# Seven block products instead of eight for half of the values and two thirds of the keys' and values' projection

## The chip, the cores and the metric

The kernel runs on one core of a Trainium2 chip. The metric is the device time of one execution in microseconds; a profiled execution lists every instruction of each engine. TensorE (PE) multiplies, VectorE (DVE) and ScalarE (ACT) do elementwise work, SyncE (SP) issues most DMAs.

## The reference

One inference step of a two-layer decoder trunk in float32: 512 prompt tokens and 8 x 4 sample tokens, 544 in all, with a model width of 1024. Layer one is a gated MLP, layer two attends to keys and values projected once. Two products matter here:

```
uv = gelu(rmsnorm(x) @ w_in)            # w_in 1024 x 4096; the last 2048 columns are the values v
v  = layernorm(v, ln_g, ln_b)           # over the 2048 columns, so after all of them are there
y  = (u * spatial(v)) @ w_out           # the mixing
...
kv = rmsnorm(h, kv_norm) @ kv_w         # kv_w 1024 x 1536: three branches of keys and values
proj = rmsnorm(h) @ b_w_in              # the queries, next after the keys
```

## The kernel before

Every float32 operand is split into a high part (ScalarE writes it, type fp32r) and a low part (VectorE subtracts the high part), and a product is three matmuls: high x high, high x low, low x high. The weights are loaded in items into two slots (`raw`), and split into `wh` and `wl`. `w_hi` and `w_ready` count high parts and finished items; `w_ready` begins at 2, so item n is finished at n + 3.

The values (lines 962 to 964) and the keys (1141 to 1143) are made token-major. `pair_b` (line 779) takes 512 columns of the weights: two items of 4 k rows, four tiles of 128 tokens, for each tile 8 k x 3 matmuls of 128x512 (line 786) into one of six PSUM banks. The 32 sample tokens go another way: four partial products in one bank (line 796), split, and gathered by a selector into bank `WIDE_GATHER` (line 805). The first half of a pair is done for all four tiles, then the second, so each tile is complete some time before the next. ScalarE scales each tile into `vt` (with Gelu) or `kvtok` (line 1669), then the few tokens (1672), then makes the high part of the next item (1653). VectorE splits (2161, the values' statistics 2192). The values have four pairs, the keys three, and the queries follow as pairs 3 and 4 with the same counters.

After the values VectorE aggregates the statistics (2351), and the mixing starts: TensorE's `mix_in` items (line 754) and `mix_spatial` (1004), VectorE's scaling (2369), finishing of `vt` (2389, 2394) and gating (2378 and `store`), ScalarE's normalising (1767). TensorE's first mixing item has in its middle the transposes of the spatial weights `wsraw` (976).

The order on every engine is written out by hand. The counters that the change touches are `f_mm` (partial products done), `wide_mm` (tiles done), `wide_free` and `wide_few` (tiles and few tokens stored), `k_sq`, `k_sd` (used for the keys' head squares).

## Time and profile before

| | us |
|---|---|
| median of 3 runs | 1540.78 |
| lowest run | 1538.75 |
| the profiled execution | 1539.93 |
| its span, from the first to the last instruction | 1538.1 |
| TensorE busy in it | 1508.9 |
| VectorE busy | 1051.4 |
| ScalarE busy | 640.4 |

In the profile an instruction's duration runs to its completion, and one may start a little before the last has ended, so the time from start to start is what an engine's queue pays. Matmuls overlap in the same way: a 128x512 one is listed with 0.39 us and the next starts after 0.23.

### The profile page before, as it was taken

To read this page: it belongs to the slowest core of one execution; us is meant where nothing else is said; L and a number is where in the kernel's file an instruction comes from. 1 tells how busy PE (TensorE), PEld (TensorE's weight loads), DVE (VectorE), ACT (ScalarE), POOL (GpSimd) and SP (SyncE) were. 2 spreads that over 40 slices of the span, in tenths; PEclk is the share of its full clock that TensorE was granted. 3 is DMA by queue.
4 is the path that set the end of the run, shared out by engine and by line. 5 is a ranking of instruction groups with operands and counts; after the bars stand their busy time and mean duration, and the time that the engine had idled before them with its cause. 6 is when DMAs were issued, how large, how long until landed. Compare 5 with 4: busy or idle time off the path is not lost.

```text
span 1538.1 us, 28834 instructions
## 1 busy us (share of the span) xinstructions
PE 1508.9 (98%) x11746; PEld 1380.4 (90%) x11746; DVE 1051.4 (68%) x1567; ACT 640.4 (42%) x1067; POOL 94.5 (6%) x155
## 2 busy tenths in 40 slices
PE   9999999999999999999999999998999999999998
PEld 6779999999999999998777756776799999999998
DVE  5339753368877869756266777877668969778952
ACT  6335311233333324334344667776543334333422
POOL 0000000000000000000000125553000000000000
PEclk9999999999999999999999999999999999999999
DMA  5438222322231323232315613104542232323232
GB/s 171 159 105 300 63 83 83 100 82 83 69 121 58 124 91 95 76 110 82 110 61 159 175 57 110 56 1 140 153 121 83 69 96 83 110 69 124 81 101 69
DMA packets 127816, 157.09 MB, mean 102 GB/s; under 512 B 11930, under 2 KB 102386, under 8 KB 127282
## 3 DMA queue, kind: packets, MB, share of 16 engines
q1 hardware_dynamic: 127346, 155.29, 31.7%
q8 instruction: 83, 1.36, 0.4%
q14 instruction: 35, 0.29, 0.1%
q10 hardware_dynamic: 352, 0.15, 0.0%
HBM read 149.58 MB, written 14.16 MB: 106 GB/s over the span
## 4 chain that ended last, share of the span: by engine, by line
PE 91%; DVE 5%; ACT 2%; issue 1%; DMA 0%; POOL 0%; SPq 0%; DVEq 0%; ACTq 0%
PE PS L754 40%; PE PS L1067 21%; PE PS L786 13%; PE PS L1383 2%; PE PS L1398 2%; PE PS L1300 2%; PE PS L1355 1%; PE PS L796 1%; PE PS L1263 1%; PE PS L1004 1%; PE PS L1366 1%; DMA xtok<-in_x_prompt 0%; PE PS L1518 0%; PE PS L1495 0%; PE PS L1461 0%
## 5 line engine op out<-in xcount | busy, mean ns | idle before, releaser
L2161 DVE TENSOR_TENSOR wl<-raw,wh 128x2048 fp32r<-128x2048 f32 (+2 forms) x89 | 167.9, 1887 | 128.4 <-ACT wh L1653 85.1
L1633 ACT ACTIVATE wh<-raw 128x2048 fp32r<-128x2048 f32 (+2 forms) x73 | 110.4, 1513 | 227.7 <-PE PS L754 140.5
L2212 DVE TENSOR_TENSOR hT<-PS,hT 128x544 f32<-128x544 f32 (+1 forms) x104 | 75.1, 722 | 130.4 <-PE PS L754 130.0
L1067 PE MATMUL PS<-opL,whA 128*128 128x272 f32 x512 | 148.7, 290 | 0.0
L1067 PE MATMUL PS<-opH,whA 128*128 128x272 f32 x512 | 147.8, 289 | 0.4 <-DVE wlB L2477 0.4
L1067 PE MATMUL PS<-opH,wlA 128*128 128x272 f32 x512 | 147.8, 289 | 0.0
L754 PE MATMUL PS<-act0h,wh 128*128 128x272 f32 x640 | 133.5, 290 | 0.4 <-DVE sg L2369 0.4
L754 PE MATMUL PS<-act0l,wh 128*128 128x272 f32 x640 | 132.3, 288 | 0.0
L754 PE MATMUL PS<-act0h,wl 128*128 128x272 f32 x640 | 132.3, 288 | 0.0
L1067 PE MATMUL PS<-opL,whB 128*128 128x272 f32 x384 | 111.5, 290 | 0.0
L1067 PE MATMUL PS<-opH,wlB 128*128 128x272 f32 x384 | 110.8, 289 | 0.0
L1067 PE MATMUL PS<-opH,whB 128*128 128x272 f32 x384 | 110.7, 288 | 0.0
L754 PEld LDWEIGHTS PS<-act0h,wh 128*128 128x128 f32 x640 | 100.5, 188 | 0.8 <-issue 0.5
L754 PEld LDWEIGHTS PS<-act0h,wl 128*128 128x128 f32 x640 | 100.3, 188 | 0.0
L754 PEld LDWEIGHTS PS<-act0l,wh 128*128 128x128 f32 x640 | 100.3, 188 | 0.0
L1067 PEld LDWEIGHTS PS<-opH,whA 128*128 128x128 f32 x512 | 96.7, 189 | 0.8 <-DVE wlB L2477 0.8
L1067 PEld LDWEIGHTS PS<-opH,wlA 128*128 128x128 f32 x512 | 96.5, 189 | 0.0
L1067 PEld LDWEIGHTS PS<-opL,whA 128*128 128x128 f32 x512 | 96.2, 188 | 0.0
L754 PE MATMUL PS<-f1h,wh 128*128 128x272 f32 x448 | 92.8, 288 | 0.0
L754 PE MATMUL PS<-f1h,wl 128*128 128x272 f32 x448 | 92.8, 289 | 0.0
L754 PE MATMUL PS<-f1l,wh 128*128 128x272 f32 x448 | 92.4, 288 | 0.0
L786 PE MATMUL PS<-wh,act0h 128*128 128x512 f32 x224 | 89.4, 399 | 1.1 <-DVE act0l L2312 1.1
(416 smaller groups left out, 3688.6 us busy)
## 6 DMA issues: line engine op xcount, KB each, us to landing
raw<-in_ffn_w_gate SPq DMA_DIRECT2D x44, 512.0 KB
raw<-in_ffn_w_up SPq DMA_DIRECT2D x44, 512.0 KB
raw<-in_a_w_in SPq DMA_DIRECT2D x32, 512.0 KB, 4.7
raw<-in_ffn_w_down SPq DMA_DIRECT2D x64, 256.0 KB
raw<-in_a_w_out SPq DMA_DIRECT2D x16, 512.0 KB
crows<-in_cache_kv_cmp SPq DMA_DIRECT2D x32, 256.0 KB, 2.9
cache<-in_state_kv_win SPq DMA_DIRECT2D x8, 1024.0 KB, 7.5
out_kv_win_sample<-in_state_kv_win SPq DMA_DIRECT2D x8, 1016.0 KB
```

The lines of the kernel that those rows point to most:

```text
L754: mm = pe.matmul(PS[:, 4 * ps + 2 * mt + h, 0:HALF], W[:, rs, k, mt * P:mt * P + P], Xp[:, k * T + h * HALF:k * T + h * HALF + HALF], star ...
L786: return pe.matmul(PS[:, wide_bank(QT * w + t), :], Xp[:, a:a + P], wide(W, k // 4)[:, k % 4, :], start=(k == 0 and W is wh and Xp is xh), ...
L796: mm = pe.matmul(PS[32 * j:32 * j + 32, WIDE_FEW, :], few[:, 4 * half + j, :], wide(raw, half)[:, j, :], start=(half == 0), stop=(half == 1))
L1004: pe.matmul(PS[:, 4 + 2 * mt, ch * P:ch * P + P], vt[:, ch, f0:f0 + P], wsT[:, g, :], start=False, stop=(ch == QT - 1))
L1067: mm = pe.matmul(PS[:, bank, 0:HALF], w, X[:, x, k, :], start=(k == 0 and not last and X is opH), stop=(k == 3 and last))
L1263: tr = pe.transpose(PS[:, 2 * (m % 2) + p, pg * P:pg * P + P], rows, ident)
L1300: mm = pe.matmul(PS[:, 4 + y % 2, 0:n], W2[:, y % 2, l, :], x[:, :, l, :], start=(l == 0), stop=(l == 7))
L1383: tr = pe.transpose(PS[:, 5 + n % 3, c0 + kt * P:c0 + kt * P + P], probs_at(v, g2)[:, kt * P:kt * P + P], ident)
L1398: mm = pe.matmul(PS[64 * g2:64 * g2 + 64, 4, 0:P], kvtok[:, kt, c0:c0 + HD], turned_at(v, g2)[:, kt * P:kt * P + P], start=(br == 0 and kt ...
L1633: act.activation(wh[:, rs, 0:kn, :], raw[:, rs, 0:kn, :], ACT.Copy).then_inc(w_hi, 1)
L2161: dve.tensor_tensor(wl[:, rs, 0:kn, :], raw[:, rs, 0:kn, :], wh[:, rs, 0:kn, :].bitcast(F32), ALU.subtract).then_inc(w_ready, 1)
L2212: dve.tensor_tensor(h, psum_u(s, mt), h, ALU.add).then_inc(free[s], 1)
```

## The change

The last 1024 columns of the values (pairs 2 and 3) and of the keys' projection (pairs 1 and 2) become one `unit` each: a 512 x 1024 by 1024 x 1024 product, cut into 2 x 2 blocks (256 tokens by 512 k, 512 k by 512 columns), made with seven block products in Winograd's form instead of eight. `unit_b` does them on TensorE as items 0 to 7; the product with the fourth input sum is done as two half items, 4 and 5.

- Four sums of input blocks (`unit_sums_made`, VectorE; high parts `unit_sums_high`, ScalarE; low parts `unit_sum_low`, VectorE). The sums are made ahead: for the values after the first pair's splits, for the keys ahead of the first.
- Four sums or differences of weight blocks, called T1 to T4 after their counter values, made by VectorE in place in `raw` and in two more buffers (`r2`), then split as items.
- Seven joins on VectorE that add results in PSUM to what stands in `vt` or `kvtok`: U2, U4, C12, C22, U3, C11, C21. Product 0 is copied out by ScalarE. ScalarE then applies Gelu (or the scaling) in place to the joined blocks.
- The unit's weights: block 0 in four DMAs, a second block into `r2`, a third into slot 1, and the last one after product 3's operand is split. The load of `wsraw` is moved behind the first two mixing items.
- The few tokens keep partial products and gathers, with the same numbers; the first four are issued inside the pair ahead (`unit_first_few`), the next eight write the gather bank and so wait for `wide_few`.
- The counters of items, `k_sq` and `k_sd` are shifted for everything later.

```diff
-    at_v = plan.take(8, 0)
+    at_v = plan.take(12, 0)
...
+    unit_v = unit_of(at_v[0] + 4, 2 * QT, 4, 2, 4, 0, vt, 1024, 0, few_v, part_v, sel_v,
+                     (A_P1, A_P1 + 8192, A_P2 + 17408, A_P2 + 25600), r2_at(0, A_P1 + 16384, A_P1 + 20480), (2, 4, 0))
+    unit_k = unit_of(at_kv[0] + 2, V_TILES + QT, 10, 5, 10, 1, kvtok, 512, 32, few_k, part_b, sel_b,
+                     tuple(A_V + 8192 * j for j in range(4)), r2_at(1, A_P2 + 30720, A_SG), (4, 2, 0))
...
+        def unit_blocks(u, w, c):
+            sp.wait_ge(w_ready, u.item + 1)
+            sp.wait_ge(f_mm, u.few_mm - 1)
+            block([wide(raw, 0)[:, k:k + 1, :] for k in range(4)], w, 0, c, loaded[0], 64)
+            block([x[:, :, :] for x in u.r2], w, 0, c + 2 * CW, s_first, 32)
+            sp.wait_ge(w_ready, u.item + 2)
+            sp.wait_ge(f_mm, u.few_mm)
+            block([wide(raw, 1)[:, 2 * j:2 * j + 2, :] for j in range(2)], w, 4, c + 2 * CW, loaded[1], 32)
+        def unit_last_block(u, w, c):
+            sp.wait_ge(w_ready, u.item + 3 + 3)
+            sp.wait_ge(f_mm, u.few_mm + 3)
+            block([wide(raw, 1)[:, 2 * j:2 * j + 2, :] for j in range(2)], w, 4, c, loaded[1], 96)
...
+        def unit_first_few(u):
+            pe.wait_ge(w_ready, u.item + 3)
+            for j in range(4):
+                mm = pe.matmul(PS[32 * j:32 * j + 32, WIDE_FEW, :], u.few[:, j, :], wide(raw, 0)[:, j, :], start=True, stop=False)
+            mm.then_inc(f_mm, 1)
...
+            def product(item, X, bank, ks=range(4), slot=0, after=None):
+                pe.wait_ge(w_ready, u.item + item + 3)
+                s = item % 2
+                for t in range(2):
+                    for k in ks:
+                        for Xp, W in ((X[0], wh), (X[0], wl), (X[1], wh)):
+                            mm = pe.matmul(PS[:, bank + t, :], Xp(k, t), wide(W, s)[:, k - slot, :],
+                                           start=(k == 0 and W is wh and Xp is X[0]), stop=(k == 3 and Xp is X[1]))
+                    if t == 0 and after is not None:
+                        after()
+                mm.then_inc(wide_mm, 1)
...
+            pe.wait_ge(s_first, u.second + 64)
+            pe.wait_ge(wide_few, u.few_n)
+            partials(WIDE_GATHER, 0, lambda j: u.r2[j // 2][:, j % 2, :], True)
+            pe.wait_ge(loaded[1], 32 * u.item + 64)
+            partials(WIDE_GATHER, 1, lambda j: wide(raw, 1)[:, j, :], False)
+            pe.wait_ge(wide_free, u.stored - (u.item == unit_v.item) * QT)
+            product(0, block(0, 0), a)
+            pe.wait_ge(wide_free, u.stored)
+            product(1, made(0), b)
+            product(2, made(1), c)
+            pe.wait_ge(wide_free, u.stored + 1)
+            product(3, made(3), a, after=lambda: gather(0))
+            pe.wait_ge(k_sq, u.joins + U4)
+            product(4, made(2), b, ks=range(2))
+            product(5, made(2), b, ks=range(2, 4), slot=2)
+            pe.wait_ge(loaded[1], 32 * u.item + 256)
+            partials(WIDE_FEW, 1, lambda j: wide(raw, 1)[:, j, :], False)
+            product(6, block(1, 0), c)
+            pe.wait_ge(k_sq, u.joins + U3)
+            product(7, block(1, 1), b, after=lambda: gather(1))
...
-        for w in range(4):
-            pair_b(w, at_v, (act0, few_v, part_v, sel_v), 0, 0, 0,
-                   *((first_values, values_split, values_few) if w == 0 else ()))
+        pair_b(0, at_v, (act0, few_v, part_v, sel_v), 0, 0, 0, first_values, values_split, values_few)
+        pair_b(1, at_v, (act0, few_v, part_v, sel_v), 0, 0, 0, ahead=unit_v)
+        unit_b(unit_v)
...
+            pe.wait_ge(k_sq, unit_v.joins + C21)
             pe.wait_ge(wide_few, 4)
             spread_and_turn()
-        pe.wait_ge(wide_free, V_TILES - 2)
+        pe.wait_ge(k_sq, unit_v.joins + C11)
...
-        for w in range(3):
-            pair_b(w, at_kv, (act0, few_k, part_b, sel_b), 8, V_TILES, 4,
-                   *((first_keys, keys_split, keys_few) if w == 0 else ()))
+        pair_b(0, at_kv, (act0, few_k, part_b, sel_b), 8, V_TILES, 4, first_keys, keys_split, keys_few, ahead=unit_k)
+        unit_b(unit_k)
...
+        def unit_sums_high(u):
+            act.wait_ge(k_sq, u.joins + MADE)
+            for j in range(4):
+                ins = act.activation(u.S[j][0][:, :, :], u.x_sum[j], ACT.Copy)
+            ins.then_inc(k_sd, 1)
...
+            act.wait_ge(k_sq, u.joins + T1)
+            unit_split(u, 1, r0, 0)
+            few_high(WIDE_GATHER, u.few_mm + 3)
+            act.wait_ge(k_sq, u.joins + T2)
+            unit_split(u, 2, r0, 1)
+            act.wait_ge(f_lo, u.few_mm + 2)
+            act.activation(u.dst[:, 0:2, c1:c1 + 512], PS[:, a:a + 2, :], ACT.Copy).then_inc(wide_free, 1)
+            act.wait_ge(loaded[1], 32 * u.item + 64)
+            unit_split(u, 3, r1, 2)
+            act.wait_ge(k_sq, u.joins + T3)
+            act.wait_ge(wide_mm, u.tiles + 3)
+            act.activation(wide(wh, 0)[:, 0:2, :], u.r2[0][:, :, :], ACT.Copy).then_inc(w_hi, 1)
+            act.wait_ge(wide_mm, u.tiles + 4)
+            act.activation(wide(wh, 1)[:, 0:2, :], u.r2[1][:, :, :], ACT.Copy).then_inc(w_hi, 1)
+            act.wait_ge(loaded[1], 32 * u.item + 256)
+            unit_split(u, 6, r1, 5)
+            few_stored(0, c2)
+            stored(C12, 0, c2, 2)
+            few_high(WIDE_FEW, u.few_mm + 4)
+            act.wait_ge(k_sq, u.joins + T4)
+            act.wait_ge(wide_mm, u.tiles + 6)
+            for j in range(2):
+                ins = act.activation(wide(wh, 1)[:, 2 * j:2 * j + 2, :], u.r2[j][:, :, :], ACT.Copy)
+            ins.then_inc(w_hi, 1)
+            stored(C22, 1, c2, 2)
+            after(0)
+            stored(C11, 0, c1, 2)
+            few_stored(1, c1)
+            stored(C21, 1, c1, 1)
+            after(1)
...
+                if u is not None and p == pairs - 1:
+                    act.wait_ge(loaded[0], 32 * u.item + 256)
+                    act.wait_ge(wide_done, 2 * (p0 + p) + 1)
+                    act.activation(wide(wh, 0), wide(raw, 0), ACT.Copy).then_inc(w_hi, 1)
+                else:
+                    wide_split(0, at[0] + 2 * p + 2, wide_done, 2 * (p0 + p) + 1)
+                if u is not None and p == pairs - 1:
+                    unit_sums_high(u)
...
+            for k0 in range(0, 4, 2):
+                for k in range(k0, k0 + 2):
+                    for n, (i, j) in enumerate(((1, 1), (0, 0))):
+                        link.put(dve.tensor_scalar(u.x_part[:, 2 * (k - k0) + n, :], x(i, j, k), g(j, k), None, ALU.mult))
+                link.settle()
+                for k in range(k0, k0 + 2):
+                    fused(s1, 1, 0, k, u.x_part[:, 2 * (k - k0), :], ALU.add)
+                    fused(s3, 1, 0, k, u.x_part[:, 2 * (k - k0) + 1, :], ALU.subtract)
+                link.settle()
+                for k in range(k0, k0 + 2):
+                    fused(s2, 0, 0, k, s1[:, k, :], ALU.subtract)
+                link.settle()
+                for k in range(k0, k0 + 2):
+                    fused(s4, 0, 1, k, s2[:, k, :], ALU.add)
+                link.settle()
+            dve.memset(small[:, 1, 3:4], 0.0).then_inc(k_sq, 1)
...
+            unit_sum_low(u, 0)
+            dve.wait_ge(f_mm, u.few_mm + 1)
+            dve.wait_ge(s_first, u.second + 64)
+            dve.wait_ge(w_ready, u.item + 3)
+            for j in range(2):
+                half = dve.tensor_tensor(r0[:, 2 * j:2 * j + 2, :], u.r2[j][:, :, :], r0[:, 2 * j:2 * j + 2, :], ALU.subtract)
+            half.then_inc(k_sq, 1)
+            low(1, r0)
+            dve.wait_ge(w_ready, u.item + 4)
+            dve.wait_ge(loaded[1], 32 * u.item + 64)
+            joined(r0, r0, r1, ALU.subtract, T2)
+            unit_sum_low(u, 1)
+            few_low(WIDE_GATHER, u.few_mm + 2)
+            low(2, r0)
+            for j in range(2):
+                half = dve.tensor_tensor(u.r2[j][:, :, :], u.r2[j][:, :, :], r1[:, 2 * j:2 * j + 2, :], ALU.subtract)
+            half.then_inc(k_sq, 1)
+            unit_sum_low(u, 3)
+            low(3, r1)
+            unit_sum_low(u, 2)
+            dve.wait_ge(wide_mm, u.tiles + 3)
+            dve.wait_ge(wide_free, u.stored + 1)
+            joined(m2, c, m1, ALU.add, U2)
+            joined(u4, b, m2, ALU.add, U4)
+            low(4, u.r2[0][:, :, :], 2)
+            dve.wait_ge(w_ready, u.item + 4 + 3)
+            dve.wait_ge(loaded[1], 32 * u.item + 256)
+            dve.tensor_tensor(u.r2[0][:, :, :], r0[:, 0:2, :], r1[:, 0:2, :], ALU.add)
+            dve.wait_ge(wide_mm, u.tiles + 4)
+            joined(m3, a, u4, ALU.add, C12)
+            low(5, u.r2[1][:, :, :], 2)
+            dve.wait_ge(w_ready, u.item + 5 + 3)
+            joined(u.r2[1][:, :, :], r0[:, 2:4, :], r1[:, 2:4, :], ALU.add, T4)
+            low(6, r1)
+            dve.wait_ge(wide_mm, u.tiles + 6)
+            joined(u4, b, u4, ALU.add, C22)
+            joined(m2, b, m2, ALU.add, U3)
+            few_low(WIDE_FEW, u.few_mm + 4)
+            dve.wait_ge(w_hi, u.item + 7 + 1)
+            for j in range(2):
+                ins = dve.tensor_tensor(wide(wl, 1)[:, 2 * j:2 * j + 2, :], u.r2[j][:, :, :],
+                                        wide(wh, 1)[:, 2 * j:2 * j + 2, :].bitcast(F32), ALU.subtract)
+            ins.then_inc(w_ready, 1)
+            stat(1, (2,), (0, 1), 1)
+            dve.wait_ge(wide_mm, u.tiles + 7)
+            joined(m1, c, m1, ALU.add, C11)
+            split(0, u.item + 8)
+            stat(1, (2,), (2, 3), 3)
+            stat(0, (), (0, 1), 5)
+            dve.wait_ge(wide_mm, u.tiles + 8)
+            joined(m2, b, m2, ALU.add, C21)
+            stat(0, (1,), (2, 3), 7)
+            split(1, u.item + 9)
```

## Rows read from the trace of the kernel before

**Rows 1.** The page: busy time and share, then the chain by engine.

```profile
PE 1508.9 (98%) x11746; PEld 1380.4 (90%) x11746; DVE 1051.4 (68%) x1567; ACT 640.4 (42%) x1067; POOL 94.5 (6%) x155
...
PE 91%; DVE 5%; ACT 2%; issue 1%; DMA 0%; POOL 0%; SPq 0%; DVEq 0%; ACTq 0%
```

**Rows 2.** The chain of waits in the values: start us, us, engine and line.

```profile
64.42 19.65 PE PS L786 x84
...
84.53 2.80 PE PS L786 x12
...
112.11 6.04 PE PS L754 x48
```

**Rows 3.** The chain of waits, the keys and the queries.

```profile
732.52 1.85 PE PS L796 x16
...
782.07 1.85 PE PS L796 x16
...
818.28 0.49 PE PS L1162 x5
```

**Rows 4.** Busy time by stretch: length, PE, PEld, DVE, ACT, POOL, PEclk, DMA share, GB/s.

```profile
62.57:112.11 49.54, 49.54 (x230) 37.46 (x231) 17.51 (x26) 15.06 (x16) 0.00 (x0) 1.00 0.48 162
...
732.52:782.07 49.55, 49.55 (x232) 37.20 (x236) 10.37 (x6) 14.64 (x16) 0.00 (x0) 1.00 0.25 85
...
132.83:159.88 27.05, 26.64 (x216) 26.32 (x215) 26.57 (x42) 6.76 (x9) 0.00 (x0) 1.00 0.71 233
...
900.00:1000.00 100.00, 94.66 (x845) 65.11 (x843) 79.53 (x158) 66.85 (x190) 48.56 (x65) 1.00 0.25 85
```

**Rows 5.** The timeline of VectorE after the values: start us, us, instruction.

```profile
115.25 2.29 DVE L2161 TENSOR_TENSOR wl<-raw,wh 128x2048 fp32r<-128x2048 f32 x1 [0.97 <-ACT wh L1653]
...
117.46 1.99 DVE L2351 BATCH_NORM_AGGREGATE stats<-bstat 128x2 f32<-128x48 f32 x5
...
126.08 0.72 DVE L2369 TENSOR_TENSOR sg<-PS,rsb 128x544 f32<-128x544 f32 x1 [0.16 <-PE PS L754]
...
132.83 0.72 DVE L2369 TENSOR_TENSOR sg<-PS,rsb 128x544 f32<-128x544 f32 x1 [1.26 <-PE PS L754]
```

**Rows 6.** Groups of instructions, shapes kept apart: busy us, mean ns, idle before.

```profile
L2161 DVE TENSOR_TENSOR wl<-raw,wh 128x2048 fp32r<-128x2048 f32 x53 | 121.7, 2297 | 117.1 <-ACT wh L1653 85.1 <-ACT wh L1633 32.0
...
L2161 DVE TENSOR_TENSOR wl<-raw,wh 128x1024 fp32r<-128x1024 f32 x32 | 39.2, 1224 | 7.5 <-ACT wh L1633 7.5
...
L1633 ACT ACTIVATE wh<-raw 128x1024 fp32r<-128x1024 f32 x32 | 34.0, 1061 | 147.1 <-PE PS L1067 86.1 <-PE PS L754 61.0
...
L2312 DVE SCALAR_TENSOR_TENSOR act0l<-hT,gains,act0h 128x256 fp32r<-128x256 f32 x4 | 1.9, 480 | 0.0
```

**Rows 7.** The timelines of VectorE and ScalarE around the values' second pair.

```profile
53.06 2.29 DVE L2161 TENSOR_TENSOR wl<-raw,wh 128x2048 fp32r<-128x2048 f32 x1 [8.92 <-ACT wh L1653]
...
63.33 1.41 DVE L2192 BATCH_NORM_STATS2 bstat<-vt 128x6 f32<-128x256 f32 x4 [2.48 <-ACT vt L1669]
...
62.61 0.69 ACT L1669 ACTIVATE vt<-PS,stats 128x512 f32<-128x512 f32 x1 [2.54 <-PE PS L786]
...
63.19 0.68 ACT L1672 ACTIVATE vt<-PS,stats 128x512 f32<-128x512 f32 x1
```

**Rows 8.** The timelines of VectorE and ScalarE in the keys.

```profile
719.27 0.19 DVE L2285 RECIPROCAL stats<-stats 128x5 f32<-128x5 f32 x1 [0.28 <-ACT stats L1704]
...
729.54 2.29 DVE L2161 TENSOR_TENSOR wl<-raw,wh 128x2048 fp32r<-128x2048 f32 x1 [4.46 <-ACT wh L1653]
...
785.21 2.29 DVE L2161 TENSOR_TENSOR wl<-raw,wh 128x2048 fp32r<-128x2048 f32 x1 [10.38 <-ACT wh L1653]
...
727.59 1.92 ACT L1653 ACTIVATE wh<-raw 128x2048 fp32r<-128x2048 f32 x1 [3.33 <-DMA raw<-in_kv_w]
```

**Rows 9.** DMA issues of the first 140 us: KB each, median us to landing.

```profile
raw<-in_a_w_in SPq DMA_DIRECT2D x26, 512.0 KB, 4.7
...
wsraw<-in_a_w_spatial SPq DMA_DIRECT2D x1, 512.0 KB, 9.8
```

More of the change, by code:

```diff
@@ L812, in tile_free @@
                     pe.wait_ge(wide_free, i0 + i - 5)
+                if behind is not None and t % 2 == 0:
+                    pe.wait_ge(k_sq, behind.joins + (C11, C21)[t // 2])
             if first is None:
@@ new lines, in unit_wide, with few_high, few_stored, stored @@
+        def unit_wide(u, func, part, after):
+            def few_high(bank, f):
+                act.wait_ge(f_mm, f)
+                act.activation(part[0][:, :, :].rearrange("p s n -> p (s n)"), PS[:, bank, :], ACT.Copy).then_inc(f_hi, 2)
+            def few_stored(n, c):
+                act.wait_ge(wide_done, u.gathers + 2 * n + 2)
+                act.activation(u.dst[:, QT, c:c + 512], PS[:, WIDE_GATHER, :], func,
+                               scale=stats[:, C_RS + QT:C_RS + TT]).then_inc(wide_few, 1)
+            def stored(join, i, c, n):
+                act.wait_ge(k_sq, u.joins + join)
+                for t in range(2):
+                    x = u.dst[:, 2 * i + t, c:c + 512]
+                    ins = act.activation(x, x, func, scale=stats[:, C_RS + 2 * i + t:C_RS + 2 * i + t + 1])
+                    if n == 2 or t == 1:
+                        ins.then_inc(wide_free, 1)
+            a, b, c = u.banks
+            c1, c2 = u.c0, u.c0 + 512
+            r0, r1 = wide(raw, 0), wide(raw, 1)
+            act.wait_ge(k_sq, u.joins + T1)
[28 more added lines that the diff above has]
+            after(1)
@@ L1673, in segment_wide @@
                                scale=stats[:, C_RS + QT:C_RS + TT]).then_inc(wide_few, 1)
[L1674 removed]
+                if u is None or p < pairs - 1:
+                    wide_split(1, at[0] + 2 * p + 3, wide_mm, i0 + QT * p + QT)
+            if u is not None:
+                unit_wide(u, func, part, lambda s: wide_split(s, u.item + 8 + s, wide_mm, u.tiles + 7 + s))
         def none(i, s, unit, use):
@@ L2192, in value_stats, with unit_sums_made, fused @@
                     dve.bn_stats(bstat[:, t, j, :], vt[:, t, j * CW:(j + 1) * CW]).then_inc(v_stat, 1)
-        def segment_wide(at, pairs, part, f0, evac=None):
+        def unit_sums_made(u):
+            x = lambda i, j, k: hT[:, 4 * j + k, 2 * P * i:2 * P * i + 2 * P]
+            g = lambda j, k: gains[:, u.gain + 4 * j + k:u.gain + 4 * j + k + 1]
+            s1, s2, s3, s4 = u.x_sum
+            def fused(out, i, j, k, other, op):
+                link.put(dve.scalar_tensor_tensor(out=out[:, k, :], in0=x(i, j, k), scalar=g(j, k), in1=other, op0=ALU.mult, op1=op))
+            for k0 in range(0, 4, 2):
[14 more added lines that the diff above has]
+            dve.memset(small[:, 1, 3:4], 0.0).then_inc(k_sq, 1)
@@ new lines, in unit_stats, with stat @@
+        def unit_stats(u):
+            def stat(half, few, tiles, n):
+                for t in tiles + (QT,) * len(few):
+                    if t == QT:
+                        dve.wait_ge(wide_few, u.few_n + (2 - half))
+                    else:
+                        dve.wait_ge(wide_free, u.stored + min(8, n + 1 + t % 2))
+                    for j in range(2):
+                        c = u.c0 + 512 * half + CW * j
+                        dve.bn_stats(bstat[:, t, c // CW, :], u.dst[:, t, c:c + CW]).then_inc(v_stat, 1)
+            return stat
@@ L2196, in segment_wide @@
+        def segment_wide(at, pairs, part, f0, evac=None, u=None, stat=None):
             for p in range(pairs):
@@ L2200, in segment_wide @@
                     evac(p)
-                split(1, at[0] + 2 * p + 3)
+                if u is None or p < pairs - 1:
+                    split(1, at[0] + 2 * p + 3)
+                if u is not None and p == pairs - 2:
+                    unit_sums_made(u)
+            if u is not None:
+                unit_wide(u, part, stat)
         def none(i, s, unit, use):
```

107 lines of the change are left out of this document (89 added, 18 removed).

## The prediction

> **What bounds the kernel now.** I read the page first. TensorE is busy 98% of the span, and the chain of work that ended last is 91% TensorE work [rows 1]. So instructions taken from TensorE can count, but only where TensorE is what ends last. I therefore read the chain around the two places that change. In the values, from the third pair's first partial product to the end of the fourth, nothing but TensorE stands in it: 62.57 to 112.11 us [rows 2, 4]. The keys look the same from 732.52 to 782.07 us [rows 3]. But the values are followed by the gated mixing, and there the chain changes engine. From 132.83 to 159.88 us VectorE is busy 26.32 of 27.05 us and TensorE, with 26.64, idle 0.4 [rows 4]: it waits at the end of that window for the scaling of line 2369. Both engines are full there, and VectorE hands over last. After the keys TensorE waits again, at 818.28 us, but that wait starts from the end of the query pair, so it moves with TensorE [rows 3].
>
> **What is removed.** A tile pair is 4 tiles x 8 k x 3 products = 96 matmuls; 84 take 19.65 and 12 take 2.80 us [rows 2], 0.2337 us each. Two pairs are 192. The unit does seven block products of 2 x 4 x 3 = 24, that is 168, each 24 x 0.2337 = 5.61 us. The partial products (1.85 us a pair [rows 3]) and the gathers stay as many as before. So each unit takes 5.61 us off TensorE, 11.2 us for both. That is 0.7%; all that follows is how much of it stays.
>
> **What is added, with prices.** VectorE: a 128x1024 subtraction takes 1.22 us, and 1.15 from start to start, since one of 2048 columns takes 2.29 and lets the next start after 2.21; ScalarE's high part takes 1.06 or 1.92 [rows 5, 6, 8]. The unit has on VectorE four low parts of input sums, four weight sums of 2 x 1.15 (T1 to T4), five full-size splits (one of them in halves), two of half size for the fifth product, which is done as items 4 and 5, seven joins of 1.15 with about 0.1 for their own wait, and two few-token parts of half that. No row shows a join of two PSUM banks; the nearest is the subtraction of the same size, and I take it. The input sums need eight tensor_scalar and sixteen fused operations; a fused one of 256 columns takes 0.48 us [rows 6], 0.40 from start to start. With 0.3 to 0.4 for a tensor_scalar (no row at this size; not above the fused one) and eight settles that is some 9.5 us. They lie in VectorE's idle 8.92 us before 53.06 [rows 7] and, for the keys, from 719.46 to about 729 us, where VectorE next splits at 729.54 anyway [rows 8]. They cost nothing there. Without that cover they would add what runs over. ScalarE's four high parts of input sums are 4 x 1.0 us. For the values they push back the storing of tiles that nobody waits for.
>
> **The values' unit, step by step.** The second pair now holds four partial products for the unit (0.92 us) and ends at 63.5. The next partials write the gather bank, so TensorE waits for wide_few: ScalarE stores tile 3 and then the few tokens, 1.3 us after the pair's end (62.61 to 63.87 in the trace) [rows 7]. **Stall 1.3.** Partials 1.85 and product 0 end at 72.3. VectorE, done with its statistics 2.1 us after the pair's end [rows 7], does the low part of sum 0 (1.15), T1 (2.3), waits for ScalarE's high part (1.9) and splits (2.21): ready at 73.4. **Stall 1.2.** Product 2 needs T2 (2.21), high part (1.9), split (2.29), a serial 6.5 us against 5.61 of cover: **stall 0.9.** Products 3, 4 and 5 come without one; the late block, asked for when product 3's operand is split, lands 5.2 us later (an issue, then the 4.7 that such loads took [rows 9]) in time for T4. Product 6 waits for ScalarE's high part, which may start only when product 4 has freed the slot (1.8 + 2.2 us against 2.8 + 0.9): **stall 0.6.** The unit ends at 112.11 - 5.61 + 4.0 = 110.5.
>
> But VectorE leaves it with a backlog. From the split of product 7's operand on it has no gap: split 2.2, six bn_stats at 0.35 [rows 7], join C11 1.15, split 2.2, ten more bn_stats, join C21. C21 ends at 114.4, although product 7 ended at 110.5. ScalarE then stores C21's two tiles, 1.3. Six bn_stats and a split follow and end at 120.15. (One statistic, the few-token rows of the upper half, is taken twice: 22 instead of 20, 0.7 us.) The aggregation that starts at 117.46 in the trace [rows 5] starts at 120.15, **2.7 us later**. Behind it VectorE ran to 132.83 with waits for TensorE of 0.16 and 1.26 us only [rows 5]; those absorb 1.4. The end of the VectorE chain moves from 159.88 to 161.2. TensorE, free earlier, waits for the triangle masks and bias rows instead. So the values' unit **costs 1.3 us**: its gain goes into waits inside it and in the mixing. Bounds: if VectorE had no backlog its chain would begin some 3 us earlier than now and the 1.4 us of waits count too, -4.5; with 3 us more backlog, +4.5. I take +1.3 because each link has a row.
>
> **The keys' unit.** The only pair before it is the first, whose tiles ScalarE stores late. The high part of block 0 waited for its load to 727.59 [rows 8]; now four issues instead of two, about 0.9 us more. Then come 1.8 us of high part, 4 us of high parts of the sums, four tiles and the few tokens at 0.58: wide_few at 737.6. TensorE, ready after 732.52 + 0.92 = 733.4, waits **4.2**. After that VectorE, without statistics, keeps ahead, and only product 6 stalls (0.6). The unit ends at 782.07 - 5.61 + 4.8 = 781.3. VectorE leaves it at 787.9 against 785.21 + 2.21 = 787.42 [rows 8], and still has its low parts ready when the next pair's end calls for them, so the queries move with TensorE: **-0.8**. Bounds: -5.6 with all hidden; +1.5 if the wait on the stored few tokens is 2.3 longer.
>
> **The rest.** The mixing weights (wsraw) load later, behind the unit's last block and two items, about 104 us; they took 9.8 us to land among other loads [rows 9], so 114, before TensorE's 116.5. If that cover is gone, each us late adds to the same point, where VectorE has the last word anyway. SP has no queue behind the unit's blocks but ln_gb and small constants, all used in the mixing.
>
> Sum against the profiled execution: 1539.93 + 1.3 - 0.8 = 1540.4 us; the median of the runs is 0.85 us above that execution, so **1541.3 us**.
>
> **A rule weighed.** In every stretch, even from 900 to 1000 us where TensorE was idle 5.3%, the granted clock is 1.00, the 2.4 GHz level [rows 4]. The Trainium skill, "TensorE: Matmul & The Clock Gate", section "HAM oscillation — how this bites in real kernels", says that waits between groups of matmuls can send the clock back down. By that rule the longest pause could slow what follows it, and the sum would be that of rival D, 1581; by the rows nothing is added.
>
> **Rivals.** (A) The forecast: the two stalls at the hand-over to a unit and VectorE's backlog take nearly all, 1541.3. For it: VectorE's 26.32 of 27.05 us after the values. Chance 0.64.
> (B) The work hides: the few tokens are stored sooner than I count, or VectorE's pieces overlap, and both units keep most of their bound, -4.5 and -5.6 with part lost: 1540.8 - 8 = 1533. For it: VectorE is busy only 17.5 of 49.5 us in the values now and 10.4 in the keys [rows 4]. Against it: the added work more than doubles that. Chance 0.19.
> (C) The serial chains are longer: every hand-over of a weight sum costs another 0.5 to 1 us, at seven products twice, part of it hidden: about +6 on A, 1547. Against it: the durations are all of operations of the same shape. Chance 0.13.
> (D) Slower by over 2%, one mechanism: the 4.2 us wait at the keys' unit lets the clock fall to 1.2 GHz. A unit at half clock costs 168 x 0.2337 = 39.3 us more, 1581; it decides the verdict from 132 matmuls (30.8 us) on. Against it: the clock stayed at 1.00 through stretches with more idle time in all [rows 4]. Chance 0.03.
> The rule of the Trainium skill's page cited above would give this rival.
> (E) Something outside the two units speeds up by more than the 11.2 us they can give. No row supports it: 0.01. That the unit does not do fewer products is excluded by the loop bounds.
>
> **Numbers.** The likeliest is A, 1541.3. The range from B to C, 1533 to 1547, leaves out D, E and the tails of B and C, under 2 in 10. A change of 2%, 31 us, is about what a measurement of this kernel can tell from none. Both units together can give 11.2, so faster by over 2% is E, 0.01; slower is D, 0.03; within 2% is 0.96.
>
> **What would show it.** In the changed kernel's trace: L786-like matmuls fewer by 48 with the same 0.234 us pitch; a wait of 1.3 us before the first partials of the values' unit and of 3 to 4 us before the keys'; stalls of about 1 us before products 1 and 2 of the values only; TensorE leaving the values near 110.5 us; VectorE's aggregation (line 2351's successor) starting near 120 and not 117.5; the first TensorE work after the mixing's VectorE chain near 161; the keys ending 0.8 us less than the shift so far. I am wrong if VectorE's aggregation starts at or before 117.5, if the keys' first wait is under 2 us, or if the granted clock is under 1.00 anywhere.

## The result and the profile after

| | before | after |
|---|---|---|
| median of 20 runs, us | 1540.25 | 1542.32 |
| the profiled execution, us | 1539.93 | 1544.5 |
| its span, us | 1538.1 | 1542.7 |
| TensorE's busy time, us | 1508.9 | 1503.7 |
| VectorE's busy time, us | 1051.4 | 1128.8 |

The ratio of after to before is 1.0017, with a 95% interval of 1.0011 to 1.0024: 2 to 3 us slower, far inside 2%. The forecast was 1541.3. (One of before's 20 runs took 6100 us; it does not move the median.) TensorE has 48 matmuls fewer, and their 11.2 us came back as waits and, in part, as slower matmuls. After's page, the busy time by engine and the chain by engine, beside [rows 1]:

```profile
PE 1503.7 (97%) x11698; PEld 1372.9 (89%) x11698; DVE 1128.8 (73%) x1665; ACT 661.6 (43%) x1087; POOL 95.0 (6%) x155
...
PE 88%; DVE 8%; ACT 3%; issue 1%; DMA 0%; POOL 0%; SPq 0%; DVEq 0%; ACTq 0%
```

TensorE's busy time fell by 5.2 and not by 11.2 us, though 48 matmuls are gone. What that means is read from the timeline and the clock. First the values: the timeline of TensorE, of which only the rows after a wait are shown, and the first row behind the mixing's chain (start us, us, line, and in brackets the idle time and what ended it).

```profile
65.00 1.06 PE L950 MATMUL PS<-second,few_v 128*32 128x512 f32 x8 [1.45 <-ACT vt L1876]
...
73.66 0.47 PE L941 MATMUL PS<-wh,s00h 128*128 128x512 f32 x1 [0.99 <-DVE wl L2447]
...
80.17 0.50 PE L941 MATMUL PS<-wh,s01h 128*128 128x512 f32 x1 [0.79 <-DVE wl L2447]
...
99.37 0.50 PE L941 MATMUL PS<-wh,act0h 128*128 128x512 f32 x1 [0.56 <-DVE wl L2447]
...
125.72 0.69 PE L1112 MATMUL PS<-wsT,early 4*32 4x32 f32 x16 [0.62 <-DVE wsT L2731]
...
134.28 0.47 PE L1126 MATMUL PS<-bsr,pick 128*128 128x512 f32 x1 [1.68 <-DVE bsr L2747]
...
161.26 0.49 PE L807 MATMUL PS<-act0h,wh 128*128 128x272 f32 x2
```

The first four waits are the unit's own. The next two are in the mixing and end with VectorE. In before TensorE had no wait at all between 108 and 145 us. VectorE's timeline says why: from the split at 107.89 to the aggregation it has one gap, 1.47 us, in which ScalarE stores the joined tiles.

```profile
107.89 2.29 DVE L2368 TENSOR_TENSOR wl<-raw,wh 128x2048 fp32r<-128x2048 f32 x1
110.10 3.36 DVE L2518 BATCH_NORM_STATS2 bstat<-vt 128x6 f32<-128x256 f32 x10
113.38 1.21 DVE L2441 TENSOR_TENSOR vt<-PS,vt 128x1024 f32<-128x1024 f32 x1
116.05 2.06 DVE L2518 BATCH_NORM_STATS2 bstat<-vt 128x6 f32<-128x256 f32 x6 [1.47 <-ACT vt L1819]
118.03 2.27 DVE L2368 TENSOR_TENSOR wl<-raw,wh 128x2048 fp32r<-128x2048 f32 x1
120.22 1.99 DVE L2683 BATCH_NORM_AGGREGATE stats<-bstat 128x2 f32<-128x48 f32 x5
```

The aggregation is at 120.22, in [rows 5] at 117.46: 2.76 us late. The first TensorE work after the mixing's chain is at 161.26 us, in before at 159.88. The keys' first partial products start at 722.94, in before at 721.59: +1.35. The two executions differed already ahead of the unit: the second pair's first partial products, which the change doesn't touch, start at 37.76 us in before and at 37.53 in after. From there the aggregation is 2.99 us late and the values cost 1.58.

Now the keys. ScalarE's high part of block 0 starts when the load has landed, in [rows 8] at 727.59:

```profile
730.49 1.92 ACT L1864 ACTIVATE wh<-raw 128x2048 fp32r<-128x2048 f32 x1 [4.88 <-DMA raw<-in_kv_w]
```

The timeline of TensorE at the hand-over to the keys' unit:

```profile
734.78 1.07 PE L915 MATMUL PS<-raw,few_k 128*32 128x512 f32 x8 [0.91 <-DVE wl L2368]
739.22 1.94 PE L950 MATMUL PS<-second,few_k 128*32 128x512 f32 x8 [3.37 <-ACT kvtok L1876]
740.89 1.96 PE L950 MATMUL PS<-raw,few_k 128*32 128x512 f32 x8
742.79 0.80 PE L941 MATMUL PS<-wh,act0h 128*128 128x512 f32 x1
743.38 0.63 PE L941 MATMUL PS<-wl,act0h 128*128 128x512 f32 x1
...
749.44 0.39 PE L941 MATMUL PS<-wh,s10h 128*128 128x512 f32 x1
```

Eight partial products took 1.07 us before the long wait and 1.94 after it. The table by stretch (length; busy time of PE, PEld, DVE, ACT and POOL; granted clock; DMA share; GB/s) gives the reason:

```profile
735.00:737.00 2.00, 0.85 (x8) 0.00 (x0) 0.78 (x1) 2.00 (x4) 0.00 (x0) 1.00 0.02 7
737.00:739.00 2.00, 0.00 (x0) 0.00 (x0) 1.97 (x3) 2.00 (x4) 0.00 (x0) 0.78 0.00 0
739.00:741.00 2.00, 1.78 (x12) 0.56 (x16) 0.84 (x1) 1.20 (x2) 0.00 (x0) 0.50 0.00 0
741.00:743.00 2.00, 2.00 (x13) 0.34 (x6) 1.19 (x1) 0.81 (x2) 0.00 (x0) 0.50 0.00 0
743.00:745.00 2.00, 2.00 (x5) 1.60 (x6) 1.97 (x2) 0.57 (x1) 0.00 (x0) 0.52 0.00 0
745.00:747.00 2.00, 2.00 (x10) 1.62 (x9) 1.97 (x2) 0.00 (x0) 0.00 (x0) 1.00 0.00 0
```

During the wait the granted clock fell to 0.50, the 1.2 GHz level, and came back to 2.4 GHz at about 745 us. The sixteen partials took 3.57 us instead of 1.85 [rows 3]; the next matmuls start 0.43 us apart instead of 0.23, and product 0 takes 6.65 us to product 1's first matmul at 749.44, where `k_busy` below, at full clock, has 5.66. Together that is 2.7 us. Slower matmuls are also longer busy, which is why the busy time fell so little: in `all_three` below, at full clock and with the same matmuls, it is 1498.5 us, 10.4 less than before.

The difference of the two spans, 4.6 us, by stretches between the same instructions of the two traces:

| stretch | before | after | difference |
|---|---|---|---|
| to the values' second pair | 37.76 | 37.53 | -0.23 |
| to the keys' first partials | 683.83 | 685.41 | +1.58 |
| to the queries' partials | 60.41 | 62.44 | +2.03 |
| to the gate products after the queries | 26.61 | 27.40 | +0.79 |
| to the transposes behind them (`gT`) | 9.67 | 8.89 | -0.78 |
| to the end of a 1.6 us wait that both have, near 1070 us | 250.60 | 250.80 | +0.20 |
| to the end | 469.22 | 470.23 | +1.01 |

Behind the queries TensorE now waits at the gate products for VectorE, and in before it waited a little later for ScalarE. The timeline of TensorE there, before and after:

```profile
808.61 0.45 PE L1153 MATMUL PS<-act1h,gwh 128*48 128x272 f32 x2
...
818.28 0.49 PE L1162 MATMUL PS<-cst,gT 48*128 48x48 f32 x5 [0.71 <-ACT gT L1926]
```

```profile
812.78 0.45 PE L1282 MATMUL PS<-act1h,gwh 128*48 128x272 f32 x2 [0.72 <-DVE gwl L2973]
...
821.67 0.49 PE L1291 MATMUL PS<-cst,gT 48*128 48x48 f32 x5
```

The new wait of 0.72 us takes the place of one of 0.71, and the step costs nothing.

In the last stretch the clock fell a second time, 0.50 at 1073 to 1075 us, behind that wait of 1.61 us. The next 10 us took 1.6 us longer than in before, of which the stretch got 0.6 back. Before has the same wait, and in its profiled execution the clock stayed at 1.00. So executions differ in this, and the runs go with it: the lower the mean granted clock of a run of after, the longer it is. The medians are 1540.7 us at 0.999 (3 runs), 1541.7 at 0.998 (6), 1542.9 at 0.997 (8), then 1544.5, 1546.0 and 1548.2 at 0.996, 0.995 and 0.994, and a straight line through the 20 runs, 1.3 us for each 0.001, accounts for 0.73 of their variance. The profiled execution has a mean clock of 0.996, the middle one of the 20 has 0.997; that goes with its being 4.6 us above before's while the medians are only 2 us apart.

### The profile page after: what moved, and what is told of

Read it like the earlier page. It is cut to its first block, busy times and chain, and to the rows that moved or that the text cites. A ratio compares the mean times of both kernels' runs of the same rounds, so it can differ in the third digit from the quotient of the medians.

```text
span 1542.7 us, 28902 instructions
## 1 busy us (share of the span) xinstructions
PE 1503.7 (97%) x11698; PEld 1372.9 (89%) x11698; DVE 1128.8 (73%) x1665; ACT 661.6 (43%) x1087; POOL 95.0 (6%) x155
## 3 DMA queue, kind: packets, MB, share of 16 engines
q8 instruction: 83, 1.36, 0.4%
## 4 chain that ended last, share of the span: by engine, by line
PE 88%; DVE 8%; ACT 3%; issue 1%; DMA 0%; POOL 0%; SPq 0%; DVEq 0%; ACTq 0%
PE PS L807 40%; PE PS L1197 21%; PE PS L839 5%; PE PS L941 3%; PE PS L1512 2%; PE PS L1527 2%; PE PS L1429 2%; PE PS L1484 1%; PE PS L1133 1%; PE PS L1392 1%; PE PS L1495 1%; DVE wl L2447 1%; DVE wl L2368 1%; PE PS L1590 1%; PE PS L1647 0%
## 5 line engine op out<-in xcount | busy, mean ns | idle before, releaser
L2368 DVE TENSOR_TENSOR wl<-raw,wh 128x2048 fp32r<-128x2048 f32 (+2 forms) x83 | 154.1, 1857 | 54.2 <-ACT wh L1762 42.6
L2010 ACT ACTIVATE whA<-raw 128x1024 fp32r<-128x1024 f32 x32 | 33.9, 1061 | 134.9 <-PE PS L1197 78.8
```

Of the source, the lines that this page charges most:

```text
L2010: act.activation(whA[it.rs][:, 0:2, :, :].rearrange("p c k n -> p (c k) n"), raw[:, it.rs, :, 0:P], ACT.Copy).then_inc(v_hi, 1)
L2368: dve.tensor_tensor(wl[:, rs, 0:kn, :], raw[:, rs, 0:kn, :], wh[:, rs, 0:kn, :].bitcast(F32), ALU.subtract).then_inc(w_ready, 1)
```

## The experiments

All eight kernels compute the full result. Medians are of 6 to 12 runs; each ratio is against before, run on the same chip beside it (its medians were 1540.27 and 1540.25 us). The last column but one is the mean over the runs of their mean granted clocks; it is 0.9973 for after and 0.9992 and 0.9995 for before.

| kernel | median | ratio, 95% interval | span | clock of the runs | clock fell at |
|---|---|---|---|---|---|
| k_only | 1541.01 | 1.0004, 0.9994 to 1.0014 | 1539.2 | 0.9978 | keys |
| v_only | 1540.96 | 1.0003, 0.9994 to 1.0012 | 1539.2 | 0.9995 | nowhere |
| k_busy | 1541.82 | 1.0013, 1.0004 to 1.0022 | 1538.6 | 0.9985 | nowhere |
| k_product_first | 1539.76 | 1.0000, 0.9991 to 1.0009 | 1541.2 | 0.9994 | mixing, 1070 |
| v_tail | 1540.18 | 1.0004, 0.9995 to 1.0012 | 1537.8 | 0.9982 | keys |
| v_lows_early | 1542.36 | 1.0017, 1.0008 to 1.0026 | 1538.7 | 0.9964 | mixing, keys |
| all_three | 1537.49 | 0.9979, 0.9971 to 0.9988 | 1536.5 | 0.9997 | nowhere |
| all_and_two_loads | 1536.13 | 0.9970, 0.9958 to 0.9982 | 1535.7 | 0.9990 | at 10 to 14 us |

Span and the place where the clock fell are those of one profiled execution each; the last 3 us of a span, in which TensorE has ended, are left out.

The clock of the runs falls into order by what stands at the keys' hand-over. The kernels with the 3.4 us wait are lowest (after, k_only, v_tail, v_lows_early: 0.9964 to 0.9982), and those in which another matmul stands there or no keys' unit is made are at 0.9985 to 0.9997, though k_busy, at 0.9985, hardly stands apart. That is the sign in the runs, beside the single profiles, that the wait lowers the clock.

### One unit at a time

k_only keeps the keys' unit, and the values go back to four pairs; v_only the other way round.

```diff
 # k_only
-    at_v = plan.take(12, 0)
+    at_v = plan.take(8, 0)
...
-        pair_b(1, at_v, (act0, few_v, part_v, sel_v), 0, 0, 0, ahead=unit_v)
-        unit_b(unit_v)
+        for w in range(4):
+            pair_b(w, at_v, (act0, few_v, part_v, sel_v), 0, 0, 0, ...)
...
 # v_only: at_kv takes 6 items, three pairs for the keys, no unit_k
```

The loads, waits and counters of the unit that is left out go back to before's with it.

> Only the keys' unit; the values are made as before. My theory is that the two units cost separately: the values' unit about 1.4 us (by the end of VectorE's chain in the mixing, 161.26 against 159.88 us) and the keys' unit about 2 us (by the next pair's first partials, 785.45 against 782.07 us, less those 1.4). So this kernel should be 1 to 2.5 us over the kernel before, about 1542, with a wait of 3 to 4 us before the first partials of the unit and a granted clock under 1.00 behind it. Rival: the keys' unit by itself gains (the 0.8 us that I forecast), and only the two together cost; then it is 1539.5.

> Only the values' unit; the keys are made as before. By my theory 1.4 us over the kernel before, 1541.6, VectorE's aggregation starting near 120.2 us and no clock under 1.00. Rival: the gain of the products is kept behind the mixing after all, and the time is at or under the kernel before, 1540 or less.

v_only behaves as after's first 720 us: aggregation at 120.16, waits of 0.62 and 1.67 us in the mixing, the keys' first partials at 722.88, and the keys' stretch is 60.42 us long, as in before. The clock stayed at 1.00, and the span is 1.1 us above before's. k_only has the values as in before (the keys begin at 721.23) and the hand-over as in after: waits of 0.66 and 3.36 us, the clock at 0.50, a keys' stretch of 61.80 us and the same +0.79 to the gate products. In v_only the wait behind the queries is before's (0.72 us for `gT`), in k_only after's (0.71 us at the gate products). The clock's share in k_only's keys is 2.3 us. So the two costs are separate and each sits where its unit is. Each alone is about 1 us in the span and not to be told from nothing in the runs, which came out nearer to before than the 1 to 2.5 and the 1.4 us expected.

### Is it the pause that lowers the clock?

k_busy puts twelve matmuls, whose result is never used, into the keys' pause; k_product_first does product 0, which needs no few-token bank, ahead of the partial products that wait (`few_partials` holds their waits and the sixteen matmuls), and no longer makes it wait for the first pair's tiles.

```diff
 # k_busy, in unit_b before the wait
+            if u.item == unit_k.item:
+                for _ in range(12):
+                    pe.matmul(PS[:, a, :], block(0, 0)[0](0, 0), wide(wh, 0)[:, 0, :], start=True, stop=True)
             pe.wait_ge(wide_few, u.few_n)
 # k_product_first
+            if u.item == unit_v.item:
+                few_partials()
-            pe.wait_ge(wide_free, u.stored - (u.item == unit_v.item) * QT)
+            pe.wait_ge(wide_free, u.stored - QT)
             product(0, block(0, 0), a)
+            if u.item == unit_k.item:
+                few_partials()
```

> The changed kernel with twelve matmuls of 128x512 put into TensorE's queue where it waits for the stored few tokens before the keys' unit; they write a bank that the unit's first product starts afresh, and change no output. 12 x 0.234 = 2.8 us of work inside a wait of 3.4. If the fall of the clock to half comes from that pause, it stays at 1.00, the unit's sixteen partial matmuls take 1.85 us instead of 3.6 and its first product 5.6 instead of 6.3: 2.4 us less than the changed kernel, near 1540. Rival: the waits alone cost the time and the clock's fall hides in other waits; then this is within 0.5 us of the changed kernel's 1542.3. Second rival: the clock falls anyway, for some other reason than the pause; then the granted clock is 0.50 at the same place.

> The changed kernel with the keys' unit's first block product ahead of its partial products, which wait for the gather bank. The product needs only its split operand, ready at 734.7 us in the changed kernel's trace, and ran from 742.8. Both the wait of 3.4 us and the clock's fall should go, and a new wait of about 1.7 us come before the second product, whose operand VectorE finishes at 744.1: 4 us less than the changed kernel, about 1538.3. Rival: the second product's operand is what counts and it moves later, since the few tokens' split is behind the partial products on ScalarE; then the gain is only 1 to 2 us, 1541.

The timeline of TensorE in k_busy, and its clock by stretch:

```profile
734.21 1.06 PE L915 MATMUL PS<-raw,few_k 128*32 128x512 f32 x8 [0.24 <-DVE wl L2371]
735.20 2.99 PE L964 MATMUL PS<-wh,act0h 128*128 128x512 f32 x12
738.64 1.06 PE L950 MATMUL PS<-second,few_k 128*32 128x512 f32 x8 [0.45 <-ACT kvtok L1879]
739.49 1.07 PE L950 MATMUL PS<-raw,few_k 128*32 128x512 f32 x8
...
739.00:741.00 2.00, 2.00 (x18) 0.78 (x11) 0.27 (x1) 1.70 (x1) 0.00 (x0) 1.00 0.00 0
```

The partials begin 0.68 us earlier after the keys' first ones than in after, no more, but at 1.06 us each eight they are at full clock. The keys' stretch is 59.05 us against 62.44: 2.7 by the clock and 0.68 by an earlier landing of block 0, which the edit doesn't touch. (The expectation had read product 0 in after as 6.3 us, and so the clock's share as 2.4.) So the fall is the pause's and not something that a unit's matmuls bring about. In the runs the gain did not show: 1541.82 against 1542.32 is inside the spread, and within the 0.5 us that the first rival named. Their clock did rise, from a mean of 0.9973 to 0.9985, but at one and the same mean clock, 0.998, six runs of k_busy have a median of 1542.7 us and six of after 1541.7. So they lost time elsewhere than by the clock. The profiled execution, 1540.35 us, is the fastest of the 11 and can't show where; that stays open, and what the pause's clock is worth in the median is not shown by this kernel.

With product 0 first there is no wait in front of the partials at all; two of 0.79 us, ahead of products 1 and 2, are new. The timeline of k_product_first:

```profile
736.08 1.06 PE L915 MATMUL PS<-raw,few_k 128*32 128x512 f32 x8 [0.16 <-DVE wl L2373]
742.85 1.06 PE L950 MATMUL PS<-second,few_k 128*32 128x512 f32 x8
743.73 1.04 PE L950 MATMUL PS<-raw,few_k 128*32 128x512 f32 x8
745.56 0.47 PE L941 MATMUL PS<-wh,s10h 128*128 128x512 f32 x1 [0.79 <-DVE wl L2452]
```

The keys' stretch is 58.45 us, 4.0 below after's: 2.7 is the clock's, 0.8 comes from a block 0 that landed sooner than in after, which leaves 0.5 for the order by itself, since part of the wait comes back ahead of products 1 and 2. The median is 1539.76 us, 2.6 below after's, between the 1538.3 expected and the rival's 1541. But this profiled execution lost the clock in another place, behind the mixing's 1.65 us wait at 135 us:

```profile
134.00:136.00 2.00, 1.00 (x6) 0.94 (x7) 1.87 (x6) 1.63 (x2) 0.00 (x0) 0.94 0.80 260
136.00:138.00 2.00, 2.00 (x11) 2.00 (x11) 1.90 (x2) 0.35 (x1) 0.00 (x0) 0.50 1.17 358
138.00:140.00 2.00, 2.00 (x13) 2.00 (x13) 1.90 (x4) 0.00 (x0) 0.00 (x0) 0.70 0.83 260
```

In after, v_only and k_busy the same wait, as long, was followed by 1.00. So behind a wait of some 1.6 us the clock falls in one execution and not in another, and the values' unit has added such a wait. Over all ten profiled executions it fell behind the mixing's wait of 1.64 to 1.68 us in two of five and behind the wait near 1070 us in two of ten; behind the keys' 3.4 us it fell in four of four (after, k_only, v_tail, v_lows_early).

### Is VectorE's backlog what holds the mixing?

v_tail lets the last join go ahead of the ten statistics in front of it and takes a statistic once that was taken twice. v_lows_early makes the values' low parts of the input sums before the second pair ends, inside VectorE's idle time; the four calls inside the unit are then left out for the values.

```diff
 # v_tail
-            stat(1, (2,), (2, 3), 3)
-            stat(0, (), (0, 1), 5)
             dve.wait_ge(wide_mm, u.tiles + 8)
             joined(m2, b, m2, ALU.add, C21)
+            stat(1, (), (2, 3), 3)
+            stat(0, (), (0, 1), 5)
 # v_lows_early, in value_stats
+                if p == 1 and t in (1, 2):
+                    for j in ((0, 1), (3, 2))[t - 1]:
+                        unit_sum_low(unit_v, j)
```

> The changed kernel with two edits at the end of the values' unit on VectorE: the repeated statistic of the few tokens is gone (20 bn_stats instead of 22), and the last join C21 stands ahead of the ten statistics that delayed it. If VectorE's backlog is what moves the mixing, the join starts when the last product ends (110.5 instead of 113.4 us), ScalarE's two stores hide behind the statistics, and the aggregation starts 0.7 + 0.5 us or more earlier, at 119.0 instead of 120.2; the mixing's VectorE chain ends near 160.0 instead of 161.3. Rival: the chain in the mixing is held by something else, ScalarE's normalising for one, and its end stays at 161.

> The changed kernel with the values' four low parts of input sums taken while VectorE waits for tiles of the pair ahead (4 x 1.15 us out of its idle 1.67 + 1.25 + 3.68 us there) instead of inside the unit. The 1 us wait before the second product should go, the unit end 1.2 us earlier (109.4), and the aggregation start 1.2 us earlier, at 119.0. Rival: VectorE's backlog is made behind the unit, not in it; then the aggregation starts at 120.2 as before.

VectorE's timeline in v_tail:

```profile
110.89 1.23 DVE L2441 TENSOR_TENSOR vt<-PS,vt 128x1024 f32<-128x1024 f32 x1 [1.10 <-PE PS L941]
112.15 4.67 DVE L2518 BATCH_NORM_STATS2 bstat<-vt 128x6 f32<-128x256 f32 x14
116.74 2.27 DVE L2368 TENSOR_TENSOR wl<-raw,wh 128x2048 fp32r<-128x2048 f32 x1
118.93 1.99 DVE L2683 BATCH_NORM_AGGREGATE stats<-bstat 128x2 f32<-128x48 f32 x5
```

The join now waits for TensorE and not TensorE's results for the join; the statistics fill the time in which ScalarE stores. The aggregation is at 118.93 where 119.0 was expected, and the keys begin at 721.61 instead of 722.94. Some of that is an earlier start, since the values' second pair begins at 37.19 us here and at 37.53 in after. Counted from there, the keys begin after 684.42 us, in after after 685.41 and in before after 683.83: 1.0 of the unit's 1.6 us is gone. So VectorE's backlog holds the mixing, and the join that stands behind ten statistics and the statistic taken twice are the larger part of the cost. v_lows_early takes away the wait ahead of product 1, and its aggregation is at 118.86. Yet the keys begin at 722.95 and the median is 1542.36: nothing is gained. Its clock, by stretch:

```profile
130.00:135.00 5.00, 3.32 (x21) 2.99 (x20) 4.83 (x11) 3.89 (x5) 0.00 (x0) 0.84 1.13 364
135.00:140.00 5.00, 5.00 (x36) 5.00 (x36) 4.44 (x9) 0.00 (x0) 0.00 (x0) 0.82 0.98 312
```

The waits of the mixing are still there (0.61 and 1.68), the clock fell behind the second, and of the 1.36 us won at the aggregation nothing is left at 722.95 us. In this profile that is what took it back. The runs point the same way: none of the 11 has a mean clock above 0.997, and their mean, 0.9964, is the lowest of all kernels, 0.0009 under after's, which by after's line is 1.2 us. Why this kernel's clock falls more often is not shown.

### Together

all_three has k_product_first, v_tail and v_lows_early. all_and_two_loads also loads the unit's block 0 in two DMAs, as a pair's, and not in four:

```diff
-            block([wide(raw, 0)[:, k:k + 1, :] for k in range(4)], w, 0, c, loaded[0], 64)
+            block([wide(raw, 0)[:, 2 * j:2 * j + 2, :] for j in range(2)], w, 0, c, loaded[0], 128)
```

> The changed kernel with the edits of v_tail, v_lows_early and k_product_first together. By my accounts: aggregation at 117.8 us, the mixing's VectorE chain 2.4 us earlier than in the changed kernel (158.9, 1 us under the kernel before), the keys' stretch 58.5 us instead of 60.4, the gates' step 0.8 us longer: 2 us under the kernel before, 1538.2. With the long pause gone and the mixing's waits shorter the clock should fall as seldom as in the kernel before. Rival: the mixing's own VectorE work sets the end whatever starts it, and only the keys' gain stays, 1539.2.

> all_three with the unit's first block loaded by two DMAs instead of four. In the changed kernel's trace that block's high part waited for its load until 730.49 us, 1.5 us later than the two-DMA load of the kernel before allows for; if the number of issues is the cause, it starts 1 us earlier, the keys' stretch is 1 us shorter, and the time 0.5 to 1 us under all_three. Rival: the block was late because the next two blocks load beside it; then nothing changes.

all_three is the first version faster than before, 0.9979, with the clock at 1.00 throughout its profiled execution, the mixing's wait down to 1.50 and a keys' stretch of 59.29 us. Its aggregation is at 118.57, and this execution began the values' second pair 0.77 us later than after's (38.30): from there the aggregation comes as early as the 117.8 expected, and the keys 0.9 us sooner than in before. So without its backlog the values' unit does gain. With two loads the wait for block 0's split, 1.11 us in all_three, is gone too:

```profile
733.52 1.06 PE L915 MATMUL PS<-raw,few_k 128*32 128x512 f32 x8
740.29 1.07 PE L950 MATMUL PS<-second,few_k 128*32 128x512 f32 x8
...
742.62 0.47 PE L941 MATMUL PS<-wh,s10h 128*128 128x512 f32 x1 [0.40 <-DVE wl L2455]
```

The reason is in SyncE's time to issue block 0, first in after and then in all_and_two_loads:

```profile
724.11 1.79 SPq L600 DMA_DIRECT2D raw<-in_kv_w  x4
```

```profile
723.83 0.91 SPq L600 DMA_DIRECT2D raw<-in_kv_w  x2
```

Two more issues take 0.88 us. ScalarE started on block 0 5.01 us after the first issue here, and 4.87 and 5.22 in before and v_only, which also use two DMAs; with four DMAs for the same bytes the seven other profiled executions took 5.55 to 6.57, 5.94 in the mean. The blocks that load beside it are the same as in all_three, so they are not what made it late. The keys' stretch is 57.44 us, 3.0 below before's, and the kernel runs in 1536.13 us, a ratio of 0.9970. Its aggregation is at 120.00, since this execution was 1.43 us behind all_three's already at the values' second pair: the clock was low from 10 to 14 us. The mixing's wait is 1.50 us as in all_three.

## Why the prediction held, step by step

- **Readings.** From 132.83 to 159.88 us VectorE is busy 26.57 us; 26.32 is TensorE's weight loads, the column before it in [rows 4]. Both engines are full there all the same. The matmuls of [rows 2] come to 0.2339 us each and not 0.2337, and the terms given for the keys' stored few tokens to 737.2 us and not 737.6. None of the three moves the forecast by more than 0.4 us.
- **Products removed, prices.** 48 matmuls fewer at the same pitch. The join of two PSUM banks took 1.21 to 1.23 us, the priced 1.22, and the input sums of the values 9.5 us (43.15 to 52.62), inside VectorE's idle time as forecast.
- **The values' stalls.** Forecast 1.3, 1.2, 0.9, 0.6; measured 1.45, 0.99, 0.79, 0.56: 3.8 against 4.0.
- **VectorE's backlog.** Forecast for the aggregation 120.15, measured 120.22; for TensorE's restart 161.2, measured 161.26. The cost of 1.3 was 1.35, or 1.58 from the values' second pair on; that the moments agree to 0.1 us is in part luck, since after's execution had begun 0.23 us sooner. v_tail, with the join moved up and the repeated statistic dropped, took 1.0 of it back. The last join ended at 114.6 against 114.4.
- **The keys' load.** Forecast 0.9 us late; in after 1.55 (2.90 later in time, 1.35 of it the values'). The price was right and after's execution an unlucky one: two more issues take 0.88 us, and over the seven profiled executions with four DMAs the block is 0.7 to 1.7 us late against before, with 0.87 in the middle.
- **The keys' first wait.** Forecast 4.2 in one piece; measured 0.91 + 3.37 = 4.3, the first for the split of block 0, which I had not listed. The stall before product 6, forecast 0.6, was 0.57.
- **The clock.** This step failed. I let it add nothing and gave its fall to rival D with 0.03, at the price of a whole unit, 39 us. It fell as D and the page of the Trainium skill had it, behind the longest pause, but was back at 1.00 by 745 us. The missing case was a fall that lasts a few microseconds; its price, 2.7 us here and 1.3 to 2.3 in three other profiles, I could have bounded from the doubled pitch. "The clock stayed at 1.00 through stretches with more idle time in all" was the wrong row for it, since it counts the sum of idle time and not the longest wait. My condition "wrong if the granted clock is under 1.00 anywhere" came true.
- **The keys' sum.** -0.8 was forecast; the stretch took +2.03 in the profiled execution, outside my bounds of -5.6 and +1.5. k_busy, with the clock at 1.00, took 59.05, that is -1.36, and after's 62.44 less the clock's 2.7 is 59.73, that is -0.7: without the clock the account was near.
- **After the queries.** VectorE reached the gate's low part at 812.17 instead of 807.39, and TensorE, which waited for nothing there in before, waited 0.72 us. I had VectorE's delay of half a microsecond but not followed it past the query pair. It cost nothing: TensorE no longer waits the 0.71 us for `gT` that it waited 10 us later in before, the wait that the prediction took to move with TensorE.
- **Sum.** Forecast +0.5 over before's profiled execution, measured +4.6. Of that the two falls of the clock are 2.7 and about 1 us, which leaves some 0.9, near the 0.5. In the medians it is +2.1; the typical run has a higher clock than the profiled one. The mechanism was right, since the largest terms, some 10 us of waits against 11.2 us of work, were right, and the missing one was the clock. That the total is only 1.0 us off is in part luck: before's median over three runs, 1540.78, from which the forecast was counted, came down to 1540.25 over 20.

**The rule weighed.** The Trainium skill, "TensorE: Matmul & The Clock Gate", section "HAM oscillation — how this bites in real kernels": waits between groups of matmuls can send the clock back down. The traces agree: 0.50 behind a wait of 3.36 or 3.37 us in after, k_only, v_tail and v_lows_early, 1.00 where twelve matmuls filled it. The 1581 us that the prediction gave for this did not come, since the clock was back at 1.00 after some 7 us.

## What to carry to other kernels

Work taken from an engine that is busy 98% of the time is only worth what the next stage's hand-over lets through: follow the helper engine's queue to the point where it has the last word, and look there for a statistic or a join that stands in the wrong order. Look at the longest single wait that a change opens, not only at the sum, and put work that is ready into it: here a product moved ahead of a waiting group of matmuls went with a keys' stretch 4 us shorter in the profile, mostly by the clock, and a median 2.6 us lower. A wait that is gone in one place can be paid for in the next hand-over, and a new one can take the place of an old one, as behind the queries: compare stretches up to the next common wait. And one saving may do nothing until the others are there: v_lows_early alone gave nothing, the four edits together made the kernel 0.3% faster than before.

## What the runs showed of the hardware

- The clock's fall is short and local: from about 738 to 745 us, 2.7 us lost, and in three other profiles 1.3 to 2.3 us behind the same pause. It comes not only behind the longest pause: behind waits of 1.6 to 1.7 us (mixing, 1070 us) it fell in four of 15 cases, between executions of nearly the same instructions. The mean clock accounts for about three quarters of the variance of the runs of after, 1540.6 to 1548.2 us.
- Twelve matmuls with an unused result, 2.99 us, kept the granted clock at 1.00 where it otherwise went to 0.50.
- The same 1 MB of weights was ready for ScalarE 5.55 to 6.57 us after the first issue when four DMAs brought it (seven profiles) and 4.87 to 5.22 us when two did (three profiles); the issues took 1.79 and 0.91 us of SyncE's queue.
